# Two softmax maps combined on GpSimd in two instructions in place of one on VectorE

## What is computed

```
def diff_attend(q, k, v, q_pos, k_pos, table_b, lam, lam_init, subln):
    s = jnp.einsum('bqhmd,bkhmd->bhmqk', q, k) * B_DIM ** -0.5
    s = s + rel_bias(q_pos, k_pos, table_b)[:, None]
    p = jax.nn.softmax(jnp.where(mask, s, NEG_INF), axis=-1)
    w = p[:, :, 0] - lam * p[:, :, 1]
    o = jnp.einsum('bhqk,bkhe->bqhe', w, v)
    o = rms_norm(o, subln) * (1.0 - lam_init)
```

## Time and profile before

| | before |
|---|---|
| median of 3 executions | 3389.3 us (3381.59 to 3391.58) |
| profiled execution: its own time | 3377.82 us |
| its span, first to last instruction | 3375.7 us |
| PE busy | 3090.5 us (92%) |
| DVE busy | 1623.1 us (48%) |
| ACT busy | 1024.8 us (30%) |
| POOL busy | 22.6 us (1%), 48 instructions |
| mean granted TensorE clock | 0.960 of full speed |

### The profile page before, as it was taken

The page is one execution under the profiler, slowest core; times in us unless marked ns, Lnnn a source line. Parts: engine busy times, 40 slices in busy tenths (PEclk is TensorE's granted clock), DMA queues, the critical chain, the costliest instruction groups (busy, mean ns, idle before and its releaser), DMA issues. The chain is left out here.

```text
span 3375.7 us, 45009 instructions
## 1 busy us (share of the span) xinstructions
PE 3090.5 (92%) x17550; PEld 2831.5 (84%) x17550; DVE 1623.1 (48%) x3395; ACT 1024.8 (30%) x2037; POOL 22.6 (1%) x48
## 2 busy tenths in 40 slices
PE   6999578979799999999979987789798999999999
PEld 4888567867799999999968887678678999999998
DVE  4544268422445544544475534773225444544555
ACT  4321367542411111111143215675323111111112
POOL 0000000000000000000000000000000000000000
PEclk9999789989899999999989998899899999999999
DMA  4556786822211111111035448775401111111111
GB/s 136 137 163 185 168 189 137 186 78 113 69 38 38 46 48 38 38 56 39 7 123 145 128 147 186 176 163 143 160 23 57 57 38 38 40 55 38 38 41 59
DMA packets 405533, 317.72 MB, mean 94 GB/s; under 512 B 146962, under 2 KB 367582, under 8 KB 405290
## 3 DMA queue, kind: packets, MB, share of 16 engines
q1 hardware_dynamic: 405322, 314.86, 34.0%
HBM read 236.14 MB, written 80.46 MB: 94 GB/s over the span
## 5 line engine op out<-in xcount | busy, mean ns | idle before, releaser
L1711 DVE TENSOR_TENSOR x<-x,ffn_down 128x512 f32<-128x512 f32 x792 | 509.4, 683 | 0.0
L1733 DVE TENSOR_TENSOR ffn_xn<-ffn_xn,ffn_up 128x384 f32<-128x384 f32 x132 | 73.2, 554 | 754.9 <-ACT ffn_xn L1678 754.9
L457 PE MATMUL ffn_up<-ffn_h_hi,ffn_hi_g 128*128 128x384 f32 x1056 | 358.5, 340 | 15.8 <-DVE ffn_h_lo L260 11.2
L457 PE MATMUL ffn_up<-ffn_h_hi,ffn_hi_u 128*128 128x384 f32 x1056 | 355.2, 336 | 3.1 <-DVE ffn_lo_u L260 3.1
L458 PE MATMUL ffn_up<-ffn_h_lo,ffn_hi_g 128*128 128x384 f32 x1056 | 357.1, 338 | 0.0
L459 PE MATMUL ffn_up<-ffn_h_hi,ffn_lo_g 128*128 128x384 f32 x1056 | 357.0, 338 | 0.0
L459 PE MATMUL ffn_up<-ffn_h_hi,ffn_lo_u 128*128 128x384 f32 x1056 | 354.8, 336 | 0.0
L458 PE MATMUL ffn_up<-ffn_h_lo,ffn_hi_u 128*128 128x384 f32 x1056 | 354.8, 336 | 0.0
L457 PE MATMUL prj_front<-prj_w_hi,prj_h_hi 128*128 128x384 f32 (+2 forms) x864 | 320.2, 371 | 8.9 <-DVE prj_w_lo L260 8.9
L1678 ACT ACTIVATE ffn_xn<-ffn_up 128x384 f32<-128x384 f32 x132 | 64.9, 492 | 861.7 <-PE ffn_up L459 861.7
L458 PE MATMUL prj_front<-prj_w_lo,prj_h_hi 128*128 128x384 f32 (+2 forms) x864 | 310.5, 359 | 0.0
(11 more groups left out here) (178 smaller groups left out, 5129.3 us busy)
## 6 DMA issues: line engine op xcount, KB each, us to landing
att_kS<-between_qk SPq DMA_DIRECT2D x80, 288.0 KB
ffn_raw_g<-in_w_gate SPq DMA_DIRECT2D x44, 512.0 KB, 4.0
ffn_raw_u<-in_w_up SPq DMA_DIRECT2D x44, 512.0 KB, 5.1
ffn_raw_d<-in_w_down SPq DMA_DIRECT2D x44, 512.0 KB, 5.2
att_qS<-between_qk SPq DMA_DIRECT2D x48, 288.0 KB
prj_w_raw<-in_w_in SPq DMA_DIRECT2D x64, 192.0 KB, 2.7
scratch_mixT<-att_mixTb SPq DMA_DIRECT2D x16, 576.0 KB, 4.9
att_qS<-between_qk SPq DMA_DIRECT2D x64, 144.0 KB
```

Source lines behind the costliest of these rows:

```text
L457: pe.matmul(out, l_hi, r_hi, start=first, stop=False)
L1711: dve.tensor_tensor(x, x, down[:, (q * ND + n) % 4, :], ALU.add).then_inc(added, 1)
L1733: dve.tensor_tensor(a32[:, b, :], sg[:, b, :], up[:, b, 1, 0:384], ALU.mult).then_inc(gated, 1)
```

## The change

DVE no longer runs the combination of L1389. It computes `coef` and signals a new semaphore, `weighted`. POOL, in its loop over the groups, walks through the 18 units of each B group: it waits for `weighted`, multiplies p1 by `coef` in place (L1137), waits for that, adds p1 to p0 in place (L1139) and signals `weighed`. The wait of DVE in the sample unit stays, and now waits for POOL.

```
+    weighted, scaled_b = ph.sem("weighted"), ph.sem("scaled_b")
...
                 pool.memset(qpast[:], 0.0).then_inc(qpast_zeroed, 1)
+                if g.kind == "B":
+                    for u in range(begin[g.index], begin[g.index + 1]):
+                        n = g.n_cols(units[u][2])
+                        pool.wait_ge(weighted, before(u + 1, lambda g, h, i: g.kind == "B"))
+                        pool.tensor_scalar(p[:, u % 3, 1, 0:n], p[:, u % 3, 1, 0:n], coef[:, u:u + 1], None, ALU.mult).then_inc(scaled_b, 1)
+                        pool.wait_ge(scaled_b, before(u + 1, lambda g, h, i: g.kind == "B"))
+                        pool.tensor_tensor(p[:, u % 3, 0, 0:n], p[:, u % 3, 0, 0:n], p[:, u % 3, 1, 0:n], ALU.add).then_inc(weighed, 1)
+                        pool.wait_ge(weighed, before(u + 1, lambda g, h, i: g.kind == "B"))
...
                 if g.kind == "B":
-                    then(dve.scalar_tensor_tensor(out=coef[:, u:u + 1], in0=total[:, a:a + 1], scalar=inv[:, a + 1:a + 2],
-                                                  in1=neg_lam[:], op0=ALU.mult, op1=ALU.mult))
-                    dve.scalar_tensor_tensor(out=p[:, u % 3, 0, 0:n], in0=p[:, u % 3, 1, 0:n], scalar=coef[:, u:u + 1],
-                                             in1=p[:, u % 3, 0, 0:n], op0=ALU.mult, op1=ALU.add).then_inc(weighed, 1)
+                    dve.scalar_tensor_tensor(out=coef[:, u:u + 1], in0=total[:, a:a + 1], scalar=inv[:, a + 1:a + 2],
+                                             in1=neg_lam[:], op0=ALU.mult, op1=ALU.mult).then_inc(weighted, 1)
                     if i == TP:
                         dve.wait_ge(weighed, before(u + 1, lambda g, h, i: g.kind == "B"))
```

## The result

The changed kernel takes 3524.8 us (median of four runs, 3515.9 to 3533.8) against 3390.4 (3381.6 to 3392.0): a ratio of 1.0402 [1.0366, 1.0438], **134 us slower**. The forecast was 3416 (+27), the range ended at 3465. The profiled execution took 3530.2 us, with a span of 3528.2.

A forecast was written before the change was run, and what follows sets the result against it. It took DVE as the tightest engine in the B groups. Relief and delay cancelled in shorter units, each of eight heads lost 3.35 us at its end, 27 us in all, giving 3416 us; the range was 3386 to 3465.

The forecast's parts named there:

- I set the sum to nothing: Units of 128 to 640 columns: DVE's relief and PE's later input, about 0.6 us each way, were taken to cancel.
- forecast length: POOL's pair of multiplication and addition at 1024 columns: 3.41 us, or 3.56 with handovers, against 1.29 on DVE.
- the lag that I had named as the condition of that sum: If unit 768 were already late from the units before, the zero sum would fail, losing another 1 us a head.
- The multiplication: POOL's product of p1 by `coef`: clearing's cost plus 0.10 us, 1.05 us at 1024 columns.
- My upper bound: One POOL instruction at 1024 columns takes at most eight 128-column additions of 470 ns, 3.76 us; two take 7.5.
- The addition: POOL adding p1 to p0: 0.20 us fixed plus 2.1 ns a column, 2.36 us at 1024 columns.
- The walk through a head's end: From unit 768 to the next head's unit 256: POOL's longer combination delays each head 3.35 us, 27 us over eight.
- DVE the tightest: In the B groups DVE is busiest, 54.62 of 62 us; the change removes 57.3 us of its work.
- The clearing of `qpast` behind the pairs: It starts at about 520 instead of 512.09 but costs nothing, since SP's loads wait for a later product.
- The rival of POOL as the bound: Multiplication costs as much as addition, L(1024) is 4.9 us: +48, 3437 us; proportional cost gives 3477; chance 0.17.
- The held reduces: Rival: every DVE instruction waits while POOL reads, costing 100 us in all, 3489 us; chance 0.05.
- `coef` held by POOL: `coef`, with two SBUF inputs, waits until POOL's instruction ends: some 0.25 us a head at the sample unit, 2 us in all.

The follow-up runs named there:

- e4: The changed kernel with the eight sample units' combination back on DVE in one instruction, the 64 others staying on POOL; ratio 1.0385.
- e1: The changed kernel with 24 or 10 small bf16 products in PE's list ahead of each B unit's transposes, keeping PE busy; 3478.3 us, ratio 1.0277.
- e6: The changed kernel with POOL's multiplication on only the first third of each unit's columns, the addition in full; ratio 1.0195, +66 us.
- e7: The changed kernel with a third of the multiplication, plus 12 or 5 small bf16 products ahead of each B unit's transposes; ratio 1.0120, +41 us.
- e2: The kernel before the change, with 8 or 4 small bf16 products ahead of each B unit's transposes; ratio 1.0021, +7 us.

## Why the prediction missed

The sign and the place were right: the transposes wait for POOL (in the B groups of the first layer 36.8 us of PE's idle time stand before them, against 7.6 us put down to DVE before), and the cost arises in the B groups. Step by step:

- *"I set the sum to nothing" for the units of 128 to 640 columns, with each start taken as it was up to `coef` of unit 768: the step that failed.* DVE's first reduce of each unit marks the steps of a head in every trace. Divide a head by them into its end as it was walked (unit 1024 over the sample unit to unit 256 of the next head) and the steps between (256 to 1024). So much more than before the eight heads took, in us, in the one profiled execution of each:

| | ends of heads | steps between |
|---|---|---|
| forecast | 27 | 0 |
| after | 59 | 60 |
| e4, sample unit on DVE | 57 | 56 |
| e1, after with PE kept busy | 48 | 36 |
| e6, pair of forecast length | 38 | 21 |
| e7, e6 with PE kept busy | 30 | 14.5 |
| e2, before with PE kept busy | 2 | 10 |

In the head shown, two marks of the table (units 256 and 1024) stand in after, in e6 and in e7 at:

```profile
506.94 0.42 DVE L1385 CUSTOM_DVE_ANT_0 att_s<-att_S,att_add_p 128x256 f32<-128x256 f32 x1
533.42 1.23 DVE L1385 CUSTOM_DVE_ANT_0 att_s<-att_S,att_add_p 128x1024 f32<-128x1024 f32 x1 [0.78 <-ACT att_p L1288]
```

```profile
504.91 0.42 DVE L1385 CUSTOM_DVE_ANT_0 att_s<-att_S,att_add_p 128x256 f32<-128x256 f32 x1
528.19 1.22 DVE L1385 CUSTOM_DVE_ANT_0 att_s<-att_S,att_add_p 128x1024 f32<-128x1024 f32 x1 [0.58 <-ACT att_p L1288]
```

```profile
497.02 0.42 DVE L1395 CUSTOM_DVE_ANT_0 att_s<-att_S,att_add_p 128x256 f32<-128x256 f32 x1
516.22 1.23 DVE L1395 CUSTOM_DVE_ANT_0 att_s<-att_S,att_add_p 128x1024 f32<-128x1024 f32 x1 [0.58 <-ACT att_p L1298]
```

Half of the loss lies where the forecast had nothing, and at the forecast length it is still 21 us (e6). Two things make it up. One is the clock: I had taken PE's durations from rows at a granted clock of 1.00, but in the head shown PE ran its short units at 0.50, and keeping it busy takes the 60 us of after down to 36 (e1). The other is the lag that I had named as the condition of that sum, in units that were not late before. How much of it is left at the forecast length is not shown: of the 14.5 us in e7 a good part may be the products, which cost 10 there in the kernel before (e2).

- *The multiplication: the mis-sized term*, 1.05 against 2.85 us. I took it to be near the clearing since it reads one stream. My upper bound, eight short additions in a row, held it (3.76). The pair of 5.27 us is the sign that the forecast had named for being wrong towards slower (above 4.9). e6 has the forecast length, after the real one: 0.0402 - 0.0195 = 0.0207, 70 us of the 134 follow from this term (with some 14 us of uncertainty, and including the clock that the longer wait costs). The Trainium skill (GPSIMD Engine Reference, section Engine selection) points the same way as my guess: it calls operations with one input on GpSimd "roughly line-rate". Here the one-input multiplication is slower than the two-input addition beside it, and the measurement decides.
- *The addition*: right (2.36 against 2.34).
- *The walk through a head's end, 3.35 us a head:* near for the length that it assumed, 30 us in e7 against 27 (in single heads from 1.9 to 5.9 us, so the agreement is in part chance); at the real length it is 59. It had two ways to the same delay: DVE's wait in front of the scaling, and `take_out` behind PE's values after the transposes of unit 1024. The first wait is there (2.53 us), but e4 takes it away and the head stays as long; the second is the one that ends last.
- *What bounds: DVE the tightest.* True of before, but it told little of after: as soon as the combination sits between two engines as a slower stage, the chain through all of them counts, and relieving DVE of 57 us won nothing. Its busy time fell by only 28.6 us (1623.1 to 1594.5), where 57 were forecast. Of the missing part 14.7 us are `coef`, 30.5 us instead of 15.8.
- *The clearing of `qpast` behind the pairs costs next to nothing: right.* In after it stands behind the sample unit's pair and is done at 549.96, and SP's loads of `qpast` follow at 562.66 behind a wait of 43.6 us for PE's products, as before. It did hold DVE's scaling beside it, 1.19 us instead of 0.42. POOL's clearing and that scaling, then SP's queue:

```profile
548.99 1.19 DVE L1403 TENSOR_SCALAR att_p<-att_p,att_inv 128x384 f32<-128x384 f32 x1 [2.53 <-POOL att_p L1139]
549.01 0.95 POOL L1132 MEMSET att_qpast<- 128x1024 f32 x1
```

```profile
561.62 0.99 SPq L1097 DMA_DIRECT2D att_vp<-in_cache_b_v  x2
562.66 10.77 SPq L1105 DMA_DIRECT2D att_qpast<-between_qk_s  x16
```

- *The rival of POOL as the bound* (L = 4.9, +48) had the nearest length, 5.27, but POOL is busy only 61% of the head, and by that walk too the total would have been under half. *The held reduces* are out: 1221 ns at 1024 columns, 1219 before. *`coef` held by POOL* is seen: started at 499.48 it ends at 501.60, and POOL's addition at 499.24 + 2.34 = 501.58. The Trainium skill (SBUF — State Buffer, section Who interferes with whom) has a VectorE instruction with two inputs in SBUF contend with a GpSimd instruction that reads SBUF; this case's trace agrees. The 14.7 us of `coef` are busy time; how much of it lies on the path, where 2 were forecast, no run shows.

The account of the 134 us, then: 41 for a pair of the forecast length with the clock mostly held (e7), 25 for the clock at that length (e6 less e7, with some 9 of uncertainty), and 70 for the longer multiplication. The products' own cost stands in the first of these; e2 had 7 us for fewer of them, so the clock's share is rather larger. By the table most of the 41 lie at the heads' ends, as walked. The parts overlap: taken the other way round (e1), the clock is 42 us at the real length.

## What to carry to other kernels

When work moves to an engine that is slower at it, walk the delay through every step of the period, not only through its longest steps: half of this loss lay in the steps that were set to nothing. Ask also what TensorE does while it waits: if it goes idle at each step, price what stands behind at the low clock too, from rows of the same trace that ran at it. An operation that no row shows should be priced up to its upper bound until its form has been timed; the number of input streams was no guide to GpSimd here. And an average of busy time names the engine to relieve only as long as the relief adds no new stage to the chain.

## What the runs showed of the hardware

On GpSimd the multiplication by a factor took 2.85 us for 128 x 1024 fp32 values (0.61 us for 128 columns), 2.77 with a constant, but 1.89 as a two-tensor product with the factor broadcast; the addition took 2.34. A VectorE instruction on a single column (`coef`, 0.22 us) once lasted 2.12 us beside GpSimd's addition, and a scaling of 384 columns 1.19 instead of 0.42 us beside GpSimd's clearing. TensorE stayed at a granted clock of 0.50 through ten microseconds in which it was busy throughout, 504 to 514 us of after; with TensorE kept busy through its waits (e1), the same head ran at 1.00.
